# Expert weights of the first pair held back until the first gathered token block is in: a two-layer GLA / mLSTM step with a hierarchical mixture of experts on one Trainium2 core

## What is computed

```
for l in range(2):
    x = layernorm(alpha * x + gate * mixer(modulated x))
    h = x * (1 + scale) + shift
    # group by argmax, top 2 of its 8 experts, weights comb
    a = einsum("nd,edf->nef", h, w_gate);  u = einsum("nd,edf->nef", h, w_up)
    y = einsum("nef,efd->nd", silu(a) * u * comb[..., None], w_down)
    x = layernorm(alpha * x + gate2 * y)
```

## Time and profile before

| | |
|---|---|
| median of 3 runs | 1240.65 us (1237.39 to 1242.68) |
| the profiled execution | 1245.26 us |
| its span in the trace | 1243.5 us |
| TensorE busy | 1122.3 us (90%) |
| mean DMA rate over the span | 264 GB/s |

### The profile page before, as it was taken

One profiled execution on the slowest core, in us unless ns is written; L12 is line 12 of the kernel. 1 busy time (PEld: TensorE's weight loads), 2 busy tenths in 40 slices (PEclk: granted clock), 3 DMA queues, 4 the chain that ended last, 5 costly groups with the idle time before them and its releaser, 6 DMA issues.

```text
span 1243.5 us, 13943 instructions
## 1 busy us (share of the span) xinstructions
PE 1122.3 (90%) x4612; PEld 487.9 (39%) x4642; DVE 566.5 (46%) x1301; ACT 308.5 (25%) x553; POOL 95.8 (8%) x163
## 2 busy tenths in 40 slices
PE   4899999999589999999869999999968999999974
PEld 0444444445333333333335554544642333333322
DVE  0453232336743555555364132234674455555545
ACT  0523221302221222221124233342241121212213
POOL 4000000004210000000040000000420000000000
PEclk8899999999799999999979999999778999999988
DMA  9966548436988999999451412211576899999942
GB/s 377 370 255 264 194 192 344 185 118 237 373 323 336 398 391 398 395 382 391 177 203 34 142 61 95 94 42 77 209 288 264 348 401 399 395 395 398 364 164 90
DMA packets 51240, 328.32 MB, mean 264 GB/s; under 512 B 6144, under 2 KB 8784, under 8 KB 14464
## 3 DMA queue, kind: packets, MB, share of 16 engines
q1 hardware_dynamic: 44672, 299.92, 61.1%
q0 software_dynamic: 4912, 20.95, 4.5%
q10 hardware_dynamic: 1616, 6.93, 1.4%
HBM read 320.90 MB, written 6.88 MB: 264 GB/s over the span
## 4 chain that ended last, share of the span: by engine, by line
PE 73%; DMA 16%; DVE 5%; ACT 3%; issue 2%; SPq 1%; DVEq 0%; ACTq 0%; PEldq 0%
PE bank L686 35%; PE bank L1063 16%; DMA ring<-in_w_moe 9%; PE bank L1080 7%; PE bank L1099 4%; PE bank L1100 3%; PE bank L707 2%; DMA ring<-in_w_mod 2%; DMA ring<-in_w_out 1%; PE bank L1115 1%; PE bank L1089 1%; DMA ring<-in_w_in 1%; PE bank L1044 1%; DMA h_store<-region 1%; PE bank L1072 1%
## 5 line engine op out<-in xcount | busy, mean ns | idle before, releaser
L1063 PE MATMUL bank<-ring,region 128*64 128x512 f32 x976 | 232.1, 611 | 18.0 <-DMA ring<-in_w_moe 6.2
L686 PE MATMUL bank<-ring,hT 128*128 128x512 f32 x384 | 171.6, 599 | 1.7 <-DMA ring<-in_w_in 1.7
L1063 PEld LDWEIGHTS bank<-ring,region 128*64 128x64 f32 x976 | 76.1, 140 | 148.0 <-issue 148.0
L1080 PE MATMUL bank<-ring,region 128*64 128x512 f32 x512 | 121.4, 618 | 5.0 <-ACT region L1582 5.0
L686 PEld LDWEIGHTS bank<-ring,hT 128*128 128x128 f32 x384 | 70.9, 190 | 90.5 <-issue 89.9
L1592 ACT ACTIVATE region<-region 128x512 bf16<-128x512 f32 x60 | 37.9, 632 | 244.5 <-DVE region L2140 244.5
L2139 DVE SCALAR_TENSOR_TENSOR region<-bank,region 128x512 f32<-128x512 f32 x60 | 45.0, 751 | 112.9 <-PE bank L1080 112.8
L686 PE MATMUL bank<-ring,region 128*128 128x512 f32 x192 | 86.4, 599 | 4.7 <-ACT region L1549 1.6
L686 PE MATMUL bank<-hT,ring 128*128 128x384 f32 x256 | 87.5, 492 | 1.1 <-DMA ring<-in_w_in 1.1
L1099 PE MATMUL bank<-region 128*128 128x512 bf16 x330 | 81.0, 379 | 4.8 <-issue 4.8
L707 PE MATMUL bank<-ring,scT 128*32 128x512 f32 x384 | 53.8, 689 | 16.9 <-DMA ring<-in_w_mod 16.9
(11 more groups left out here) (321 smaller groups left out, 1234.3 us busy)
## 6 DMA issues: line engine op xcount, KB each, us to landing
ring<-in_w_moe SPq DMA_DIRECT2D x195, 1024.0 KB, 9.2
ring<-in_w_mod SPq DMA_DIRECT2D x48, 1024.0 KB, 9.7
ring<-in_w_in SPq DMA_DIRECT2D x24, 1024.0 KB, 7.5
ring<-in_w_out SPq DMA_DIRECT2D x4, 1024.0 KB, 7.4
ring<-in_w_out SPq DMA_DIRECT2D x8, 512.0 KB, 6.6
region<-gate_store POOLq DMA_DIRECT2D x4, 1024.0 KB, 6.3
region<-in_lnrows POOLq DMA_DIRECT2D x4, 1024.0 KB, 8.8
h_store<-region ACTq DMA_DIRECT2D x6, 512.0 KB, 3.2
```

Source lines behind the costliest of these rows:

```text
L686: ins = pe.matmul(out, lhsT, rhs, start=start, stop=stop, skip_group_check=True)
L1063: ins = pe.matmul(bank[6][u * CAP:(u + 1) * CAP, :], xs[:, k, u * CAP:(u + 1) * CAP], places[u][:, at:at + 2 * DE], start=k == 0, stop=k = ...
L1080: ins = pe.matmul(bank[6 + y][u * CAP:(u + 1) * CAP, :], hidT[:, f, u * CAP:(u + 1) * CAP], w, start=f == 0, stop=f == FE - 1, skip_group_ ...
```

## The change

One wait is added on SP. In each layer, after the requests for the two pieces 0 of the first pair, SP waits until gathered block 0 has landed (`rows_at[0]`), and only then requests the two pieces 1 and the two pieces 2 (4.19 MB).

```diff
                     if isinstance(i, int) and i == 0:
                         sp.wait_ge(used[1], g0)
+                        sp.wait_ge(rows_at[0], 16 * (l + 1))
                     else:
                         sp.wait_ge(S["gu_ready"], i + p0)
                     for u in range(G):
                         bring(i, u, 1)
```

## The result

The changed kernel takes 1252.99 us (median of 4 runs, 1246.57 to 1257.54) against 1239.02 for the kernel before beside it: **ratio 1.0106, 95% interval 1.007 to 1.0143**. Six further runs of it gave 1252.12 us and 1.0099 (1.0065 to 1.0134). It is slower by 12 to 13 us by these ratios; the forecast was 1239.0, no change that can be told.

What follows compares the result with a forecast made beforehand. It took layer 0 to be bound by pieces disturbing store and first gather, layer 1 by VectorE. -2.6 in layer 0 plus 1.0 in layer 1 gave -1.6 us, 1239.0 us from 1240.65; range 1234 to 1244.5.

Steps and rivals of the forecast that it cites:

- What bounds the kernel, and that the wait acts: Layer 0's start loses time to pieces delaying store and first gather; layer 1's gather waits for VectorE; the wait frees the gather.
- The disturbed store: Layer 0, third store into `h_store`: with one piece beside it, lands at about 320.0 instead of taking 9.35 us.
- Layer 0, -2.6: Layer 0, up to the first expert matmul: 346.6 in place of 349.2, a gain of 2.6 us, bounds 0.7 to 5.2.
- Layer 1, +1.0 with a bound of 3.4: Layer 1, gathers sharing engines with the four held pieces: 1.0 us lost, at most 3.4 if block 2 is late.
- What comes behind, hidden: After the gathers: late pieces 1 and later requests land before TensorE needs them, 5 us to spare; no cost.
- the gather stays disturbed: Rival: pieces follow block 0 so closely that blocks 1 and 2 stay late; gain 0.7, loss 3.4, 1243.4 us; chance 0.18.
- The moved work comes back in full: Rival: layer 1's moved 4.19 MB make the loop over the pairs start 10 us behind; 1248 us; chance 0.07.
- The Trainium skill's rule: DMA engines alternate between queue rows by packet; as equal turns, nothing lost in layer 1, sum -2.6; set against the store's 9.35 us.

Runs made afterwards that it cites:

- the second trace: The changed kernel profiled once more, with nothing changed against it; 1252.12 us, ratio 1.0099 to the kernel before.

## Why the prediction was wrong, step by step

**What bounds the kernel, and that the wait acts**: right. The first gather is undisturbed after (4.3 us to landing in layer 0 in place of the 8.79 of the earlier trace rows), and D comes earlier, 17.4 to 20.8 us after R instead of 21.1 to 22.9.

**The disturbed store** ("it lands at about 314.87 + 2.6 + 2.5 = 320.0"): wrong, and of little weight. With a single piece beside it the third store still takes 8.22 us in one trace; chain of the kernel with the wait on the sixth block:

```profile
314.16 8.22 DMA h_store<-region
```

So it is not the four pieces that were moved that make most of the 9.35 of the earlier trace rows. What the store's time does follow is the order of two requests less than 0.4 us apart: in the six traces where the second piece 0 is requested before the third store it takes 7.2 to 9.4 us, in the two where the piece comes 0.03 and 0.11 us behind the store 7.2 and 6.3, and in the six where it comes 0.22 to 0.39 us behind 3.2 to 5.0. The trace with the change in layer 1 alone is one of these, 4.3 us with all five pieces behind the store. The change does not touch this order. The first gather starts 5.9 to 6.3 us after R with the change (the forecast's 321.3 to 321.9 are 5.2 to 5.8 after R) and 5.8, 5.8, 7.1 and 8.4 without. The trace from which the gain was worked out is the 8.4: part of the stall that was to be removed is absent in the other executions.

**Layer 0, -2.6**: wrong in sign, +2.0. The step that failed is "The last gather of layer 0, the sixth, was in by 339.82, no later; so blocks 3 to 5 are not what decides." It stands under layer 1, but the sum for layer 0 rests on it too: nothing in it is put down for a wait for blocks 3 to 5. That sixth block had met only the tail of the pieces, which had gone out 7 to 10 us before the first gather. After the change they go out behind the first block and the sixth meets all of them: 14.9 to 16.9 us instead of 8.5 to 10.1. From D to E takes 14.8 to 16.0 us where I took 11.9.

**Layer 1, +1.0 with a bound of 3.4**: right in sign, mis-sized, +6.3. I priced blocks 3 to 5 at 0.166 MB/us from the mean packet sizes of the earlier trace rows over the whole span, and let block 2 be nearly through. In fact a gather gets one third, 0.14 MB/us, and from block 2 on: sixth block at 937.2, 30.4 us after R (906.8), where TensorE had wanted it 24.9 us after R in the first trace of before (928.7, R at 903.8): 5.5 us late. The first expert matmul came 28.8 us after the first gather's issue, where 24.5 was forecast. The bound of 3.4 carried one block's delay, not that of four in a row behind each other.

**The clock**: not in the sum. In layer 1 of the changed kernel TensorE's granted clock is 0.50 from 922 to 930 us, around its wait for the third block, 1.00 from 934 to 937.2, and it falls again in the short tail ahead of the experts, where TensorE is mostly idle. The first expert matmuls begin before it is back; windows of the changed kernel:

```profile
938.00:942.00 4.00, 1.32 (x8) 0.71 (x7) 1.41 (x8) 2.30 (x3) 0.00 (x0) 0.61 1.02 415
942.00:946.00 4.00, 4.00 (x12) 1.25 (x10) 0.13 (x1) 0.00 (x0) 0.00 (x0) 0.53 1.02 424
```

From 942 to 946 it is at 0.53 of full speed, that is mostly the 1.2 GHz level (0.66 from 933 to 937 at the same place before). The first 32 matmuls take 9.24 us against 8.40, and 10.02 in layer 0 of the second trace. This is inside E to A, of which 0.6 and 0.8 us are left in the mean.

**What comes behind, hidden**: right for the changed kernel. TensorE waits 2.7 us for weights in the loop of layer 0 (3.8 before) and 1.7 in that of layer 1 (2.5 before). 0.8 us of it is at the second pair of layer 0, so there nothing was left to spare: with the wait on the sixth block the same 4.19 MB did come back in layer 0.

**The rivals**: nearest in its mechanism is "the gather stays disturbed", but its price of 3.4 us was a single late block. "The moved work comes back in full" gave the nearest time, 1248, by luck: what it describes did not happen in the changed kernel.

**The Trainium skill's rule**, page "DMA: Bandwidth & Descriptors", section "Queues, rings and completion order", says that a DMA engine takes turns between its queue rows, a packet of several descriptors at a time. I had set it aside as not agreeing with the store's 9.35 us. Equal turns with unequal rows are what the blocks show (3.7 us against 8 KB rows, 2.5 to 2.6 against 4 KB, in two forms); how many rows one turn has, no run here shows. Taken with this case's row sizes, 4 and 8 KB, instead of the mean packets, it would have put the sixth block in layer 1 at 4 times 3.7 us behind the second, 935.8 (measured 937.2).

## What to carry to other kernels

Holding a large transfer back behind the first of several small ones protects the first and puts the large one on top of the rest. Wait for the last of them, and hold back no more bytes than the engines can take before they are needed: here 2.1 MB, held until the last block, gained 0.4%, and 4.19 MB lost 0.5%. Price a transfer that shares the engines by the size of its rows against the other's rows, and add the delays of all transfers behind one another on its queue, not of one. Two layers that run the same code can be bound by different things: look in each whether the stall that is to be removed is there at all.

## What the runs showed of the hardware

The two queues shared the engines by rows: 4 KB against 8 KB gave the gathers one third (381 packets against 378), 4 KB against 4 KB one half (478 against 483), the latter with DMAs of 0.52 and of 1.05 MB. DMAs into 64 of the 128 partitions kept the engines fully busy at 234 GB/s beside gathers, where DMAs into all 128 reached 420 and 423. A store of 0.52 MB into HBM took 2.6 us alone, 3.2 to 5.0 where a piece of 1.05 MB was requested 0.22 to 0.39 us after it, and 7.2 to 9.4 where the piece was requested first; why the order weighs so much stays open.
